# Hybrid GLA and retention trunk: attention in chunks of 64 tokens instead of 128, on quarters of the TensorE array

## The reference, cut to what matters

```python
def step(s, xs):                       # GLA; retention alike, with constant decays
    qc, kc, vc, lc = xs
    b = jnp.cumsum(lc, axis=2)
    qd = qc * jnp.exp(b)
    kd = kc * jnp.exp(-b)
    att = jnp.where(mask, jnp.einsum('bhtk,bhsk->bhts', qd, kd), 0.0)
    o = jnp.einsum('bhts,bhsv->bhtv', att, vc) + jnp.einsum('bhtk,bhkv->bhtv', qd, s)
    b_last = b[:, :, -1:, :]
    s_new = (jnp.exp(b_last[:, :, 0, :])[..., None] * s
             + jnp.einsum('bhsk,bhsv->bhkv', kc * jnp.exp(b_last - b), vc))
    return s_new, o
```

## Time and profile before

| | |
|---|---|
| three runs | 1651.87, 1649.62, 1651.32 us; median 1651.32 |
| the profiled execution | 1652.58 us, of which its instructions span 1650.5 us |
| busy share of the span | PE 99%, DVE 65%, POOL 51%, ACT 37% |
| mean granted TensorE clock | 0.998 of full speed |

### The profile page before, as it was taken

One profiled execution on the slowest core, in us unless ns is written; L12 is line 12 of the kernel. 1 busy time (PEld: TensorE's weight loads), 2 busy tenths in 40 slices (PEclk: granted clock), 3 DMA queues, 4 the chain that ended last, 5 costly groups with the idle time before them and its releaser, 6 DMA issues.

```text
span 1650.5 us, 26302 instructions
## 1 busy us (share of the span) xinstructions
PE 1636.9 (99%) x9792; PEld 1354.8 (82%) x9792; DVE 1070.1 (65%) x2378; ACT 617.8 (37%) x1152; POOL 834.2 (51%) x646
## 2 busy tenths in 40 slices
PE   9999999999999999999999999999999999999998
PEld 7788878888888887888878888788888888878887
DVE  5844776768764675457754367757887457784374
ACT  5414434234343343424452234342443324342342
POOL 4544545645445464445544445456554455554455
PEclk9999999999999999999999999999999999999999
DMA  8366656767455574466653656566864377553654
GB/s 290 99 112 168 195 208 153 205 192 233 144 105 153 164 198 129 127 161 160 184 149 96 163 142 190 164 189 183 189 194 135 108 169 163 173 173 99 146 154 141
DMA packets 389279, 268.18 MB, mean 162 GB/s; under 512 B 290720, under 2 KB 293152, under 8 KB 389152
## 3 DMA queue, kind: packets, MB, share of 16 engines
q1 hardware_dynamic: 315280, 131.99, 32.0%
q10 hardware_dynamic: 73872, 134.51, 26.2%
HBM read 219.34 MB, written 47.07 MB: 161 GB/s over the span
## 4 chain that ended last, share of the span: by engine, by line
PE 95%; DMA 2%; DVE 1%; SPq 1%; issue 0%; ACT 0%; ACTq 0%; POOLq 0%; POOL 0%; DVEq 0%
PE bank L781 82%; PE bank L1026 3%; PE bank L1032 2%; PE bank L986 2%; PE bank L1010 2%; DMA w_stage<-in_w_slots 1%; PE bank L875 1%; PE bank L747 1%; PE bank L807 1%; PE bank L864 0%; DMA xn<-in_x_t 0%; SPq L482 0%; DVE la L1691 0%; PE bank L909 0%; DMA k_n<-out_k_rows 0%
## 5 line engine op out<-in xcount | busy, mean ns | idle before, releaser
L280 POOL TENSOR_TENSOR w_lo<-w_stage,w_hi 128x512 fp32r<-128x512 f32 x344 | 479.1, 1412 | 472.6 <-ACT w_hi L273 472.2
L781 PE MATMUL bank<-h_hi,w_hi 128*128 128x512 f32 x1016 | 403.9, 398 | 2.5 <-ACT region L1174 1.5
L781 PE MATMUL bank<-h_lo,w_hi 128*128 128x512 f32 x1016 | 396.3, 390 | 0.0
L781 PE MATMUL bank<-h_hi,w_lo 128*128 128x512 f32 x1016 | 396.1, 390 | 0.0
L273 ACT ACTIVATE w_hi<-w_stage 128x512 fp32r<-128x512 f32 x344 | 199.7, 624 | 494.1 <-PE bank L781 437.6
L280 POOL TENSOR_TENSOR w_lo<-ss,w_hi 128x512 fp32r<-128x512 f32 x112 | 149.5, 1355 | 166.4 <-ACT w_hi L273 166.4
L781 PEld LDWEIGHTS bank<-h_hi,w_hi 128*128 128x128 f32 x1016 | 190.7, 188 | 52.0 <-issue 6.6
L781 PEld LDWEIGHTS bank<-h_hi,w_lo 128*128 128x128 f32 x1016 | 190.8, 188 | 40.5
L781 PEld LDWEIGHTS bank<-h_lo,w_hi 128*128 128x128 f32 x1016 | 190.9, 188 | 37.1
L781 PE MATMUL bank<-w_hi,m_hi 128*128 128x512 f32 (+1 forms) x520 | 201.6, 388 | 0.0
L781 PE MATMUL bank<-w_hi,h_hi 128*128 128x512 f32 x512 | 201.1, 393 | 0.0
(11 more groups left out here) (228 smaller groups left out, 2192.5 us busy)
## 6 DMA issues: line engine op xcount, KB each, us to landing
w_stage<-in_w_slots ACTq DMA_DIRECT2D x344, 256.0 KB, 3.6
ss<-in_w_slots ACTq DMA_DIRECT2D x112, 256.0 KB, 4.1
region<-in_x_prompt SPq DMA_DIRECT2D x32, 512.0 KB, 6.0
out_o_rows<-region SPq DMA_DIRECT2D x64, 256.0 KB, 3.1
v_b<-in_w_slots ACTq DMA_DIRECT2D x56, 256.0 KB, 3.0
region<-out_o_rows SPq DMA_DIRECT2D x192, 64.0 KB, 3.0
out_k_rows<-region SPq DMA_DIRECT2D x32, 256.0 KB, 3.3
k_n<-out_k_rows SPq DMA_DIRECT2D x256, 32.0 KB, 2.6
```

The costliest lines, as they stand in the source:

```text
L280: pool.tensor_tensor(w_lo[:, r, c], stage(h), w_hi[:, r, c].bitcast(f32), ALU.subtract).then_inc(lo_done, 1)
L781: i = pe.matmul(dst, x, y, start=(s == 0 and kk == 0 and c == 0), stop=(s == 3 and kk == 1 and c == 2), skip_group_check=True)
```

## The change

The kernel's chunk becomes 64 tokens (`CH`), half a tile. Each tile gets a second state in its middle (`s_half`, laid over `k_n`), and every attention product works on a 64x64 quarter of the array: z is the half of the tile, hh the parity of the head.

```diff
+CH = TOK // 2
-        SC_TWO, OUT_TWO = (ATT, OB), (ST, X)
+        SC_TWO, OUT_TWO, ST_TWO = (ATT, OB), ((ST, X), (ATT, OB)), (ST, X)
+        s_half = k_n
```

PE, per g. States go in two calls, j = 0 and 1; scores in one, on 64 columns instead of 128; outputs in one, with tiles 0 and 1 in `ST` and `X` and tiles 2 and 3 in `ATT` and `OB`:

```diff
+                    def states(g, j):
+                        if j == 1:
+                            if g == 0:
+                                pe.wait_ge(sret_sb.sem, sret_sb.at(n, 4))
+                            else:
+                                pe.wait_ge(sgla_sb.sem, sgla_sb.at(n, 7))
...
-                                    i = pe.matmul((ST, X)[t // 2][r, c:c + 128], k_n[:, t, 64 * h:64 * h + 64], v_n[:, t, 128 * h:128 * h + 128], start=True, stop=True)
+                                    for z in range(2):
+                                        h, r, kr, c = 2 * p + hh, slice(64 * hh, 64 * hh + 64), slice(CH * z, CH * z + CH), 256 * (t % 2) + 128 * p
+                                        i = pe.matmul(ST_TWO[z][r, c:c + 128], k_n[kr, t, 64 * h:64 * h + 64], v_n[kr, t, 128 * h:128 * h + 128], start=True, stop=True)
...
+                    def scores(g):
...
+                                        i = pe.matmul(SC_TWO[hh][o:o + CH, c:c + CH], k_t[r, p, part], q_two[g][r, p, part], start=True, stop=True)
...
+                    def outputs(g):
+                        pe.wait_ge(att_sb.sem, att_sb.at(n, 4 * g + 4))
+                        if g == 0:
+                            pe.wait_ge(sret_sb.sem, sret_sb.at(n, 8))
+                        else:
+                            pe.wait_ge(sgla_sb.sem, sgla_sb.at(n, 12))
...
+                                    for z in range(2):
+                                        h, kr, o, c = 2 * p + hh, slice(CH * z, CH * z + CH), CH * (z ^ hh), 256 * (t % 2) + 128 * p
+                                        i = pe.matmul(OUT_TWO[t // 2][hh][o:o + CH, c:c + 128], a_two[g][kr, t, h, :], v_n[kr, t, 128 * h:128 * h + 128], start=(t % 2 == 0 and p == 0), stop=False, skip_group_check=True)
...
+                                        r, o, c = slice(64 * hh, 64 * hh + 64), CH * (z ^ hh), 256 * (t % 2) + 128 * p
+                                        s = s_half[:, t, :] if z else s_ret if g == 0 and t == 0 else s_at[:, t, :]
+                                        i = pe.matmul(OUT_TWO[t // 2][hh][o:o + CH, c:c + 128], q_two[g][r, p, TOK * t + CH * z:TOK * t + CH * z + CH], s[r, 128 * p:128 * p + 128], start=False, stop=(t % 2 == 1 and p == 1), skip_group_check=True)
...
                         if w in (9, 17):
-                            states(g)
-                            scores_pair(g, 0)
+                            scores(g)
+                            states(g, 0)
+                        if w in (10, 18):
+                            states(g, 1)
                         if w in (11, 19):
-                            outputs_pair(g, 0)
-                            scores_pair(g, 1)
-                        if w in (12, 20):
-                            outputs_pair(g, 1)
+                            outputs(g)
```

Between the two halves of `outputs` PE waits for its own semaphore `av_ps`. The outputs of the odd heads come out with the two halves of a tile swapped (`z ^ hh`), and ACT's copies put them right, all in slot 12 (20):

```diff
+                        for j in (0, 1) if w in (12, 20) else ():
...
-                            for hh in range(2):
-                                i = nc.scalar.activation(o8[:, :, hh, :], OUT_TWO[hh][:, :].rearrange("p (a n) -> p a n", a=4), ACT.Copy)
+                            nc.scalar.activation(o8[:, :, 0, :], OUT_TWO[j][0][:, :].rearrange("p (a n) -> p a n", a=4), ACT.Copy)
+                            for z in range(2):
+                                src, dst = slice(CH * (1 - z), CH * (1 - z) + CH), slice(CH * z, CH * z + CH)
+                                i = nc.scalar.activation(o8[dst, :, 1, :], OUT_TWO[j][1][src, :].rearrange("p (a n) -> p a n", a=4), ACT.Copy)
```

DVE, per g, masks the scores in one step (two instructions of 512 elements instead of four) and adds one step to each tile's state chain:

```diff
+                                vec.tensor_tensor(s_half[:, t, :], st0, src[:, :], ALU.add).then_inc(sret_sb.sem, 1)
...
+                            vec.tensor_tensor(s_half[:, t, :], st0, s_at[:, t, :], ALU.add).then_inc(sgla_sb.sem, 1)
...
                         if w in (10, 18):
-                            scores_pair(g, 0)
-                            states(g)
+                            scores(g)
+                            states(g, 0)
+                        if w in (11, 19):
+                            states(g, 1)
                         if w in (12, 20):
-                            scores_pair(g, 1)
                             stats(g, 0)
                             stats(g, 1)
```

163 lines of the change are left out of this document (76 added, 87 removed).

## The result

| | median | runs | profiled span | PE clock |
|---|---|---|---|---|
| before | 1649.74 us | 1649.44 to 1651.87 | 1650.5 us | 0.998 |
| changed | 1631.21 us | 1630.65 to 1634.49 | 1628.8 us | 0.996 |

The account below looks back on a forecast made before the run. PE, 99% busy, was taken to bound the kernel. Attention -47.2, decode products +1.2, block run 0 -1.0 and waits +1.0 sum to -46 us: 1606.6 against the profiled execution, 1605 against the median, range 1599 to 1634.

Parts of the forecast that it names:

- rival 2: Scores times values go two at a time, as row halves write one PSUM bank: +28 us, 1633; chance 0.11.
- The forecast's own range: 1599 (lost clock comes back, a visit costs 0.35) to 1611 us; chance 0.62.
- Step and visits: PE's attention in slots 9 to 11: passes of 0.109 us, three visits of 0.35 to 0.41; 7.3 us instead of 10.25.
- rival 1: Scores don't gain from 64 columns, a pass stays at 0.109 us: +14 us, 1619; chance 0.08.
- rival 4: The array doesn't work on quarters four at a time; at two the kernel is slower by 49 us, 1700; chance 0.08.
- The +1.2 for the decode products: Decode products standing alone in block runs 0, 4, 1 and 5 cost 0.2 us each, +1.2 us.
- Block run 0, -1.0: Scores go first while PE had waited for `k_n`: -1.0 us; 1.5 us at the low clock left in.
- The margins at slots 10, 11 and 20: PE's spare time before DVE's results: 1.3 us at slot 10, 11.3 against 12.1 at slot 11, half a microsecond at 20.
- "+1.0 in all": Added waits of PE for eight GLA groups and a few crowded block runs: +1.0 us.
- Rival 3: A margin at slot 20 or 18 is used up, PE stands 1 to 2 us per GLA group: 16 us, 1621; chance 0.08.
- C: Rival explanation given after the result, not in the prediction: the clock alone causes the loss, not a wait; no chance given.

Follow-up runs that it names:

- e5: Changed kernel with ACT copying the odd heads' outputs in one 128-partition copy, swap left out (result wrong): 1623.05 us, ratio 0.9833.
- e1: Changed kernel with DVE's four transposes of the first group's outputs moved behind the second state pair of slot 19: 1627.16 us, ratio 0.9859.
- e16: e15 with POOL computing only 64 of each 512 columns of the weights' low parts (result wrong): 1605.12 us, ratio 0.9730.
- e15: Changed kernel with only DVE's and SP's order changed, including the decode's second affine step moved to slot 26: 1613.06 us, ratio 0.9770.
- e8: Changed kernel with POOL computing only 64 of each 512 columns of the weights' low parts from the seventh half slot (result wrong): 1613.38 us.
- e6: Changed kernel with four moves together: output transposes, next block's transposes and first decode affine step on DVE, decode state store on SP: 1623.86 us.
- e13: Changed kernel with the second group's outputs back in two visits, slots 19 and 20, and ACT copying the second pair in slot 21: 1627.31 us.

## Why the prediction was off

- **Where 1631 lies**: inside the range by luck. The forecast's own range ended at 1611; the stated one reached 1634 for the sake of rival 2, which did not occur.
- **Step and visits**: right. 2.17, 1.24 and 3.86 against the forecast's 7.3 in all; 64 score records in 0.98 us (484.71 to 485.69), where 0.88 was worked out. Rivals 1, 2 and 4 are refuted by the first timeline above: quarters go four at a time, on 64 columns at about half the price, and also where two row halves write one bank. The +1.2 for the decode products came as forecast: 0.2 us in each of the six slots. The rule of the Trainium skill, "TensorEngine Tiling (Array Packing)", "Gotcha 1: PSUM Pressure", behind rival 2, doesn't hold for halves in different partitions: 64 records of L1032 took 1.8 us, from 499.12 to the first product behind them at 500.92, and not 3.5.
- **Block run 0, -1.0**: there, and more. PE still waited 2.1 us for `k_n` (3.20 in the earlier trace rows), but slot 9 cost 4.51 us, 2.3 above the 2.17 of the others, where before it had cost 7.97, 4.8 above their 3.19: nearly all of the 1.5 us at the low clock, which I had left in the sum, went too. Slots 17 and 19 of the same block run lost 6.7 us.
- **The margins at slots 10, 11 and 20**: right where no transfer stood in them. States at slot 10 and outputs at slot 11 were in time in block runs 1 to 7, and so was the first `silu` at slot 21 outside of block run 1: the place that I called the tightest held.
- **"+1.0 in all"** for waits is the term that failed: PE's waits grew by 17.2 us, and with the slow products and small losses around them about 25 us of the gain are gone. I checked each engine against PE's next question and stopped at slot 21. But the 3.08 us that left slot 20 had hidden everything behind it, up to the second `silu` at slot 25 and the decode steps at slot 23. I had seen that PE comes back 3.1 us sooner and asked this of one place only.
- I also took durations for fixed. In block run 3 the last four norm instructions went from 3.06 to 5.05 us because four of POOL's splits and not two fell beside them, which is a matter of order, and is seen only by laying POOL's timeline over DVE's.
- Rival 3 was the right mechanism with 0.08 for it and 16 us; it forecast 1621 and put the waits in every GLA group, at slot 18 or slot 20. They stand in block runs 0, 1, 3, 5 and 6, and more of them at slots 23 and 25 (8.2 us with the 0.3 that 2 and 7 have each) than at the two places named.

Open is e5's gain in block run 0, and why that block run differs by up to 11 us from kernel to kernel. The link that decides at slot 25 was read for block run 3; for the decode steps at slot 23 of block runs 1 and 5 it was not. C was not tested by a run of its own; the half clock followed waits (below), and went in slot 19 with the wait in e1.

## What to carry to other kernels

When work leaves the engine that bounds a kernel, follow each chain that this work had covered to the next places where the engine asks for its results, two or three questions on and not one, in every block that carries extra work, and reckon the new start against the old. Look for the last outside link of such a chain: what is shortened ahead of it wins nothing (e5). An in-order queue is a chain: what doesn't belong to the next result (the next block's transposes, a low part that is needed a slot later) goes behind it, and moves pay together that pay nothing, or cost, alone. Where a profile has places that don't repeat, judge by the stretches that do.

## What the runs showed of the hardware

- A norm instruction of DVE that falls beside one of POOL's splits lasts as long as the split: 0.27 us alone (at 757.11), 1.33 beside a split of 1.30.

```profile
757.11 0.27 DVE L1582 TENSOR_SCALAR region<-region,rstd 128x128 f32<-128x128 f32 x1
...
763.51 1.33 DVE L1582 TENSOR_SCALAR region<-region,rstd 128x128 f32<-128x128 f32 x1
```

```profile
763.46 1.30 POOL L283 TENSOR_TENSOR w_lo<-v_b,w_hi 128x512 fp32r<-128x512 f32 x1
```

  With seven eighths of POOL's columns gone, the same DVE program was busy 234 us less: 883.5 us in e16 against

```profile
PE 1593.3 (99%) x11840; PEld 1299.2 (81%) x11840; DVE 1117.2 (69%) x2402; ACT 639.7 (40%) x1184; POOL 840.6 (52%) x646
```

  in e15. `silu`, whose one input is in PSUM, doesn't feel it: 0.68 us on average in the changed kernel, in e8 and before. The Trainium skill, "SBUF — State Buffer", "SBUF: two separate sides", describes an exclusive lock on a pair of ports, held for the whole instruction, between a GpSimd operation and a VectorE operation in a two-port mode or with two SBUF inputs. The trace agrees for DVE's side, with 1.33 against 0.27, and for `silu` with its one SBUF input; no run shows which of the two cases norm is, or POOL being held up by DVE.
- The clock after a wait. In block run 1, from the wait of 3.67 us on (PEclk is the number after POOL's count):

```profile
357.00:360.00 3.00, 0.00 (x0) 0.00 (x0) 2.78 (x22) 2.95 (x7) 1.10 (x2) 1.00 0.14 43
360.00:362.00 2.00, 1.43 (x4) 1.18 (x5) 2.00 (x4) 1.47 (x3) 2.00 (x3) 0.52 0.53 198
362.00:364.00 2.00, 2.00 (x7) 1.64 (x6) 2.00 (x3) 0.00 (x0) 2.00 (x2) 0.62 0.00 0
```

  It fell to the lower of its two levels, 1.2 GHz (0.50 of full speed, and the 2 us behind the wait have 0.52). The product behind the wait and the next five took 0.57 and then 0.43 us from start to start instead of 0.227, about 1.5 us lost in all. After the 2.61 us wait in block run 3 it stayed at 1.00; after the 2.40 us wait in block run 5 it fell (0.50 from 1180 to 1182 us), and in e6 after one of 1.97 us in block run 1 (0.53 in the 2 us behind it). So the length of the wait alone doesn't decide, and a wait of 2 to 4 us may cost 1.5 to 1.7 us more, or nothing.
- One more visit to quarters with values and queries in it costs 1.0 us and not 0.4. In e13 the queries wait for the values of the same two tiles, and the first of them starts 0.36 us behind the last value record; in the single visit these values are long done, and the first query record starts 0.09 us behind the last value record.
